# Post-FFN layer norm of a streaming encoder: where its two elementwise steps run

## The reference

```python
def layer_norm(x, g, b):
    xf = x.astype(jnp.float32)
    mu = jnp.mean(xf, axis=-1, keepdims=True)
    var = jnp.mean(jnp.square(xf - mu), axis=-1, keepdims=True)
    return ((xf - mu) * lax.rsqrt(var + LN_EPS) * g + b).astype(x.dtype)

def channel_and_ple(x, p, w13, w2, w_ple, w_gate, g, b):
    gate, up = jnp.split(x @ w13, 2, axis=-1)
    ffn = (jax.nn.silu(gate) * up) @ w2
    ple = jax.nn.sigmoid(x @ w_gate) * (p @ w_ple)
    return layer_norm(ALPHA * x + ffn + ple, g, b)
```

## Time and profile before

| | us |
|---|---|
| median of 3 runs | 3179.59 (3177.04 to 3186.04) |
| the profiled execution | 3180.57 |
| its span, first to last instruction | 3178.8 |
| TensorE busy | 3069.1 (97%) |
| VectorE busy | 1514.6 (48%) |
| ScalarE busy | 885.4 (28%) |
| GpSimd busy | 1016.3 (32%) |

### The profile page before, as it was taken

The page is one execution under the profiler, slowest core; times in us unless marked ns, Lnnn a source line. Parts: engine busy times, 40 slices in busy tenths (PEclk is TensorE's granted clock), DMA queues, the critical chain, the costliest instruction groups (busy, mean ns, idle before and its releaser), DMA issues.

```text
span 3178.8 us, 49155 instructions
## 1 busy us (share of the span) xinstructions
PE 3069.1 (97%) x19621; PEld 2881.9 (91%) x19621; DVE 1514.6 (48%) x2914; ACT 885.4 (28%) x1915; POOL 1016.3 (32%) x495
## 2 busy tenths in 40 slices
PE   8998999899999999999989999979999999999996
PEld 8697778789999999999979999967899999999996
DVE  1897855544533433333454554565444333333335
ACT  2575554342111001111134554553311111100112
POOL 3132000235633334333242222213545333333422
PEclk9998999899999999999999999989999999999998
DMA  3121000112311111111022111111222111111101
GB/s 101 28 64 38 1 1 1 41 50 81 92 46 46 46 40 53 46 46 40 14 70 58 50 43 47 40 47 54 73 89 60 52 43 45 45 46 40 53 0 55
DMA packets 209373, 149.75 MB, mean 47 GB/s; under 512 B 28914, under 2 KB 195764, under 8 KB 209236
## 3 DMA queue, kind: packets, MB, share of 16 engines
q1 hardware_dynamic: 209236, 147.85, 15.7%
HBM read 128.09 MB, written 19.73 MB: 47 GB/s over the span
## 4 chain that ended last, share of the span: by engine, by line
PE 89%; DVE 6%; issue 2%; ACT 2%; POOL 1%; DMA 0%; SPq 0%; POOLq 0%; ACTq 0%; DVEq 0%
PE psum L153 49%; PE psum L2130 16%; PE psum L1734 6%; PE psum L690 4%; PE psum L659 2%; PE psum L1322 2%; PE psum L1296 2%; DVE junk L913 2%; PE psum L671 2%; PE psum L1310 1%; PE psum L628 1%; DVE bias L872 1%; PE psum L1271 0%; PE psum L1688 0%; PE psum L1933 0%
## 5 line engine op out<-in xcount | busy, mean ns | idle before, releaser
L153 PE MATMUL psum<-x_hi,w_hi 128*128 128x352 f32 x3192 | 1039.4, 326 | 10.0 <-POOL x_lo L1677 4.1
L153 PE MATMUL psum<-x_hi,w_lo 128*128 128x352 f32 x3192 | 1026.1, 321 | 0.0
L153 PE MATMUL psum<-x_lo,w_hi 128*128 128x352 f32 x3192 | 1025.9, 321 | 0.0
L122 POOL TENSOR_TENSOR w_hi<-w_raw,zeros 128x1024 fp32r<-128x1024 f32 (+1 forms) x209 | 381.2, 1824 | 1514.6 <-PE psum L153 952.8
L153 PEld LDWEIGHTS psum<-x_hi,w_hi 128*128 128x128 f32 x3192 | 600.1, 188 | 12.2 <-issue 11.4
L153 PEld LDWEIGHTS psum<-x_lo,w_hi 128*128 128x128 f32 x3192 | 601.2, 188 | 0.5
L153 PEld LDWEIGHTS psum<-x_hi,w_lo 128*128 128x128 f32 x3192 | 599.7, 188 | 0.5
L124 POOL TENSOR_TENSOR w_lo<-w_raw,w_hi 128x1024 fp32r<-128x1024 f32 (+1 forms) x209 | 486.0, 2325 | 16.4
L2391 DVE TENSOR_TENSOR gate<-psum,gate 128x352 f32<-128x352 f32 x120 | 63.0, 525 | 725.3 <-PE psum L153 725.3
L2130 PE MATMUL psum<-h_hi,w_hi 128*128 128x352 f32 x1056 | 340.8, 323 | 1.2 <-DVE h_lo L2413 1.0
L2130 PE MATMUL psum<-h_lo,w_hi 128*128 128x352 f32 x1056 | 338.3, 320 | 0.0
(11 more groups left out here) (461 smaller groups left out, 4100.7 us busy)
## 6 DMA issues: line engine op xcount, KB each, us to landing
w_raw<-in_ffn_w_dram SPq DMA_DIRECT2D x132, 512.0 KB
w_raw<-in_b_w_in_dram SPq DMA_DIRECT2D x24, 512.0 KB
w_raw<-in_ple_w_gate_dram SPq DMA_DIRECT2D x16, 512.0 KB
x_nat<-in_x_prompt_dram SPq DMA_DIRECT2D x8, 512.0 KB, 7.6
w_raw<-in_a_w_in_dram SPq DMA_DIRECT2D x8, 512.0 KB
w_raw<-in_a_w_in_dram SPq DMA_DIRECT2D x16, 256.0 KB
x_rows<-x_rows SPq DMA_DIRECT2D x8, 512.0 KB, 2.8
out_new_b_v_prompt_dram<-valsB SPq DMA_DIRECT2D x8, 512.0 KB, 3.4
```

The costliest lines, as they stand in the source:

```text
L122: nc.gpsimd.tensor_tensor(c.w_hi[s][:, 0:kc], c.w_raw[s][:, 0:kc], zero, ALU.add).then_inc(c.split[s], 1)
L153: last = c.nc.tensor.matmul(out, w, x, start=(n == 0), stop=(n == 3 * len(terms) - 1))
```

## The change

The norm's elementwise work is arranged differently. Instead of (x/sd - mean/sd) * gain + shift in three passes on three engines, VectorE computes ((x - mean) * gain) from the PSUM rows in one scalar_tensor_tensor (`centered`), and then (that * 1/sd) + shift in a second one (`finished`), which follows its reciprocal. -mean/sd isn't computed any more; ScalarE's `normal` and GpSimd's `shifted` are gone. `centered` doesn't need the root. What `normal` waited for (the store of the buffer's last rows, and in layer 0 the turning back of tile t - 3) `centered` waits for now, on VectorE. PSUM places are free when `centered` is done (`s_gn`). In layer 1, tiles 7 and 8 get PSUM places of their own (banks 4 and 5, 6 and 7), so that TensorE turns them without a wait for an earlier tile, and tile 8 gets a fourth row buffer. The small buffers for statistics go from two to four. In the written order, `centered` and `finished` take the places of `coefs` and `gained`, with the last tiles in a slightly different order.

```diff
     def turn_bank(t):
+        if last_one and t > 6:
+            return 4 if t == 7 else 6
         return 2 if t in (5, 7) else 0
...
-        if before is not None:
-            pe.wait_ge(s_n, b_n + before + 1)
+        if before is not None and not (last_one and t > 6):
+            pe.wait_ge(s_gn, b_gn + before + 1)
...
     def stats(v, t):
-        n, j = rows(t), t % 2
+        n, j = rows(t), t % 4
         v.wait_ge(s_tr, b_tr + t + 1)
+        if t >= 4:
+            v.wait_ge(s_x, b_x + t - 3)
...
-        if t >= 2:
-            v.wait_ge(s_n, b_n + t - 1)
...
-    def coefs(v, t):
+    def centered(v, t):
+        n, j = rows(t), t % 4
+        v.wait_ge(s_mv, b_mv + t + 1)
+        if t >= 3 and not (last_one and t == QT):
+            v.wait_ge(s_out[t % 3], b_out + 16 * (t // 3))
+            if not last_one:
+                v.wait_ge(s_bt, t - 2)
+        nc.vector.scalar_tensor_tensor(out=xt[t][0:n, :], in0=c.psum[0:n, 512 * turn_bank(t):512 * turn_bank(t) + D],
+                                       scalar=mv[0:n, j, 0:1], in1=gain[0:n, :], op0=ALU.subtract,
+                                       op1=ALU.mult).then_inc(s_gn, 1)
+
+    def finished(v, t):
+        n, j = rows(t), t % 4
         v.wait_ge(s_sd, b_sd + t + 1)
         nc.vector.reciprocal(coef[0:n, j, 1:2], coef[0:n, j, 0:1]).then_inc(s_co, 1)
-        v.wait_ge(s_co, b_co + 2 * t + 1)
-        nc.vector.scalar_tensor_tensor(out=coef[0:n, j, 2:3], in0=mv[0:n, j, 0:1], scalar=-1.0,
-                                       in1=coef[0:n, j, 1:2], op0=ALU.mult, op1=ALU.mult).then_inc(s_co, 1)
-
-    def normal(act, t):
...
-    def gained(v, t):
...
-    def shifted(g, t):
...
+        v.wait_ge(s_gn, b_gn + t + 1)
+        v.wait_ge(s_co, b_co + t + 1)
+        nc.vector.scalar_tensor_tensor(out=xt[t][0:n, :], in0=xt[t][0:n, :], scalar=coef[0:n, j, 1:2],
+                                       in1=shift[0:n, :], op0=ALU.mult, op1=ALU.add).then_inc(s_x, 1)
...
@@ attention B, VectorE's order in layer 0 @@
         late.stats(v, 5)
         late.stats(v, 6)
-        late.coefs(v, 5)
+        late.centered(v, 5)
         late.low(v, 4)
-        late.coefs(v, 6)
-        late.gained(v, 5)
+        late.centered(v, 6)
+        late.finished(v, 5)
         late.stats(v, 7)
-        late.gained(v, 6)
-        late.coefs(v, 7)
-        late.gained(v, 7)
+        late.finished(v, 6)
+        late.centered(v, 7)
+        late.finished(v, 7)
         late.low(v, 5)
         project(0, K, 0)
         late.stats(v, 8)
         late.low(v, 6)
-        late.coefs(v, 8)
-        late.gained(v, 8)
+        late.centered(v, 8)
+        late.finished(v, 8)
         late.low(v, 7)
...
@@ feed-forward block, VectorE's order in the last pair @@
         added_last(2, (0,))
-        coefs(v, 4)
+        centered(v, 4)
         added_last(2, (1, 2))
-        gained(v, 4)
+        finished(v, 4)
         added_last(2, range(3, 8))
         if last_one:
             stats(v, 5)
             stats(v, 6)
-            coefs(v, 5)
-            coefs(v, 6)
-            gained(v, 5)
+            centered(v, 5)
+            finished(v, 5)
+            centered(v, 6)
             stats(v, 7)
-            gained(v, 6)
-            coefs(v, 7)
+            finished(v, 6)
+            centered(v, 7)
             stats(v, 8)
-            gained(v, 7)
-            coefs(v, 8)
-            gained(v, 8)
+            finished(v, 7)
+            centered(v, 8)
+            finished(v, 8)
```

More of the change, by code:

```diff
@@ L1863, in ffn_norm @@
     gate = c.at("gate" + tag, [P, 2, TOK], F32, 43008)
-    xt = [c.at(f"x_rows{j}_{tag}", [P, D], F32, (51456, 55552, 0)[j]) for j in range(3)]
+    row_tiles = [c.at(f"x_rows{j}_{tag}", [P, D], F32, (51456, 55552, 0, 4096)[j]) for j in range(3 + last_one)]
+    xt = [row_tiles[3 if last_one and t == QT else t % 3] for t in range(T)]
     gain, shift = c.at("gain_rows" + tag, [P, D], F32, 76032), c.at("shift_rows" + tag, [P, D], F32, 80128)
-    part = c.at("ln_part" + tag, [P, 2, 2, 6], F32, 84224)
-    mv, coef = c.at("ln_mv" + tag, [P, 2, 2], F32, 84352), c.at("ln_coef" + tag, [P, 2, 4], F32, 84384)
+    part = c.at("ln_part" + tag, [P, 4, 2, 6], F32, 84224)
+    mv, coef = c.at("ln_mv" + tag, [P, 4, 2], F32, 84416), c.at("ln_coef" + tag, [P, 4, 2], F32, 84448)
     S = lambda n: c.shared_sem("ffn_" + n)
@@ L2012, in ffn_norm @@
         late = c.late = Core()
-        late.turn, late.back, late.stats, late.root, late.coefs = turn_rows, turn_back, stats, root, coefs
-        late.normal, late.gained, late.high, late.low, late.rows_stored = normal, gained, high, low, rows_stored
+        late.turn, late.back, late.stats, late.root, late.centered = turn_rows, turn_back, stats, root, centered
+        late.finished, late.high, late.low, late.rows_stored = finished, high, low, rows_stored
         late.outputs_summed = lambda eng: eng.wait_ge(s_da, added(2, KC - 1))
@@ L2088, in pool @@
             split_unit(c, g, "attnB", 0, 1, KC)
-        for t in range(2, T):
-            shifted(g, t)
     def tensor(pe):
@@ L2304, in scalar @@
         root(act, 0)
-        normal(act, 0)
         high_last(0, 1)
         root(act, 1)
-        normal(act, 1)
         silu_last(1, 1)
@@ L2327, in scalar @@
         root(act, 4)
-        normal(act, 4)
         if last_one:
@@ L2331, in scalar @@
             root(act, 6)
-            for t in (5, 6):
-                normal(act, t)
-                root(act, t + 2)
-            normal(act, 7)
-            normal(act, 8)
+            root(act, 7)
+            root(act, 8)
     def vector(v):
@@ L2426, in vector @@
         stats(v, 0)
-        coefs(v, 0)
+        centered(v, 0)
         product_last(0, 1)
-        gained(v, 0)
+        finished(v, 0)
         low_last(0, 1)
         stats(v, 1)
-        coefs(v, 1)
-        gained(v, 1)
+        centered(v, 1)
+        finished(v, 1)
         if not last_one:
@@ L2441, in vector @@
         stats(v, 2)
-        coefs(v, 2)
+        centered(v, 2)
         product_last(0, 2)
-        gained(v, 2)
+        finished(v, 2)
         low_last(0, 2)
         stats(v, 3)
-        coefs(v, 3)
-        gained(v, 3)
+        centered(v, 3)
+        finished(v, 3)
         if not last_one:
```

29 lines of the change are left out of this document (6 added, 23 removed).

## The result

The changed kernel took 3164.44 us, median of 6 runs (3162.14 to 3166.22), against 3176.59 (3174.81 to 3186.04, 6 runs) for the kernel before: ratio 0.9950, 95% interval 0.9938 to 0.9962. The profiled execution took 3163.77, its span is 3162.0. The forecast was a gain of 13.3 us (0.42%); this comparison's ratio says 0.50%, some 16 us, its two medians 12.2 us (0.38%).

What follows compares the result with a forecast made beforehand. TensorE was taken as the bound (89% of the chain of waits). Layer 1's tail 8.5 us plus layer 0's hand-over 4.8 made 13.3 us, from a median of 3179.59 to 3166.3 us, range 3162 to 3173.

Steps and rivals of the forecast that it cites:

- What bounds, and the two places: TensorE carries 89% of the chain; the change acts only at layer 1's tail and layer 0's hand-over to attention B.
- The price of a pass: Each new VectorE pass of 1024 columns: 1.20 us start to start, 1.28 to its end, no PSUM surcharge.
- Part 1, the tail: End of layer 1: VectorE runs one unbroken queue, last norm pass ends at 3167.75 instead of 3176.22, gain 8.5 us.
- Part 2 (a): Layer 0, turning back tile 2: TensorE no longer waits for GpSimd's shift, 3.26 us of idle time go.
- (b): Layer 0, tile 3 turned back some 3.3 us earlier; the down product starts 2.8 us earlier.
- (c): Layer 0's down product: VectorE's queue stalls TensorE 1.0 us against 0.4, leaving 2.2 us of gain.
- (d): Layer 0, tile 5 to attention B's projection: 1.0 us less wait, 1.6 us by avoiding low clock, 2.6 us.
- microsecond of scatter between medians: Allowance used for the range 3162 to 3173, which was to take in R2 and R1.
- R1: Layer 0 gives nothing, through VectorE's longer queue or GpSimd's port collisions: gain 8.5 us, time 3171.1; chance 0.18.
- R2: Layer 0 gives nearly all its idle times hold, some 8 us: gain 16.5, time 3163; chance 0.12.
- R3: Slower: passes run at half rate; at 0.7 us more each the gain is gone, high end 3190; chance 0.05.
- R4: Another wait holds `centered` and TensorE's turns of tile 7 still wait: some 4 us gain, 3175.6; chance 0.07.

Runs made afterwards that it cites:

- e1: Changed kernel's norms and PSUM places in layer 1 only, layer 0 as in the kernel before: 3176.14 us, ratio 0.9991 to the kernel before.
- e2: Changed kernel's norms in layer 0 only, layer 1 as in the kernel before: 3174.63 us, ratio 0.9987 to the kernel before.
- e3: Changed kernel with the old PSUM places for tiles 7 and 8 of layer 1: 3166.34 us, ratio 0.9971 to the kernel before.
- x1: Kernel before, with layer 1's shift pass moved from GpSimd to VectorE behind the gain pass: 3180.00 us, one execution; tail 23.07 us.
- a1: Changed kernel again, no edit, in a second comparison: 3173.74 us, ratio 0.9969 to the kernel before.
- x2: Kernel before, with only the change's PSUM places for layer 1's last tiles: 3177.26 us, one execution; tail 24.81 us.
- a2: Changed kernel once more, no edit, in a third comparison: 3167.36 us, ratio 0.9963 to the kernel before.
- x3: Changed kernel plus an unneeded GpSimd pass beside each of tiles 5 to 8 in layer 1's tail: 3167.95 us, one execution; tail 22.87 us.
- x4: Changed kernel with another VectorE order in layer 0's attention B (finished of 5 and low of 5 earlier): 3170.72 us, one execution.
- x7: Same kernel as x6, timed in several runs: 3167.44 us, ratio 0.9939 to the kernel before.
- x5: x4 with 13 filler identity transposes on TensorE in place of the 1.42 us wait: 3159.99 us, one execution.
- x6: x4 with the tail's finishing of tiles 5 and 6 given to ScalarE and GpSimd: 3159.98 us, one execution; tail 14.99 us.

## Why the prediction was right, and where not

**What bounds, and the two places.** Right. Of the sections with touched code the tail and layer 0 alone moved by more than 0.15 us, and e1 and e2 show them one by one.

**The price of a pass.** Right. Both passes take 1.28 us and let the next start after 1.20. The step from reciprocal to `finished` was 0.20 to 0.26 us, forecast 0.18. No PSUM surcharge: `centered` (PSUM input) and `finished` (SBUF) take the same 1.28. My 544 ns for 512 more columns set a PSUM row beside an SBUF row of another length, so that by itself it couldn't have shown a surcharge.

**Part 1, the tail.** Right: 8.5 forecast, 8.3 measured, and 17.46 against the 17.3 that I gave as a check. The adds around tile 4's passes lost nothing (49.45 against 49.57). The claim that the places let VectorE run unbroken was wrong in its reason: e3 has the old places and the same tail. The row with 2.33 us was a collision, as said (x1).

**Part 2 (a).** Right: `finished` of tile 2 was held by the weight split, and TensorE didn't wait for it. VectorE's timeline, layer 0, against the gain pass of the earlier trace rows:

```profile
1589.08 2.39 DVE L1978 SCALAR_TENSOR_TENSOR x_rows<-x_rows,ln_coef,shift_rows 128x1024 f32<-128x1024 f32 x1
```

**(b).** Counted from X0, the down product starts 49.01 us in before (1607.69) and 45.60 after (1601.72): 3.4 earlier, forecast 2.8. The wait before tile 3's turning back is 1.47 (forecast about 1.0).

**(c).** Forecast 2.2 left at the end of this product; measured 57.80 - 55.14 = 2.7. From the down product's start to the last add it is 8.79 before and 9.54 after, 0.75 of new stall where I had 0.6.

**(d).** This is the step that failed. It had 2.6 us: 1.0 of waits and 1.6 of low clock that I took to be gone because TensorE's idle time fell from 2.44 to 1.75 us. Measured from the last add to T: 40.42 before, 39.65 after, 0.8. The waits, 1.82 + 2.44 + 1.42 before, are 1.63 + 1.90 + 1.42: 0.7 less, so that term is near. Up to V2 I am right even in size (30.93 to 28.58, 2.35; counted from X0, V2 comes 5.0 us earlier, forecast 4.8). But 1.6 us came back between V2 and T (9.49 to 11.07), one wait further on, so the 1.6 was worth nothing. In a1, the same kernel, the low clock sits where it did before:

```profile
1634.57 1.86 PE L1942 MATMUL psum<-ident,x_rows 128*128 128x128 f32 x8 [1.89 <-DVE x_lo L1993]
```

and V2 to T is 9.49; the sum is 94.9, against 94.8. All four profiles with the old layer 0 (before, e1, x1, x2) paid it behind the same wait of 2.44 or 2.45 us. The six with the changed one (the changed kernel, a1, a2, e2, e3, x3) paid it too: a1 behind the wait of 1.89 us, the other five one wait on, behind that of 1.42. So the shorter wait mostly moved the fall and never took it away. x4 and x7 paid it once as well, x5 and x6 not at all. I had read a cause into a single execution. Layer 0 gave 3.4 and not 4.8.

**The sum and the range.** 13.3 forecast, 11.8 by sections, of which the low clock explains 1.6: step (d) lost 1.8 and the tail 0.2, steps (b) and (c) gave 0.5 more. The comparison that came first said 0.50%, more than the trace can find in the touched code, and the next two 0.31 and 0.37%. The step behind this is my "microsecond of scatter between medians": single executions of one kernel lie from 3157 to 3177, and six runs fall into one group or the other. The first median, 3164.44, lies within my range of 3162 to 3173; a1's, 3173.74, of the same kernel doesn't, and that the first came so near to my 3166.3 is in part luck. Whatever the forecast's centre, a range from the terms of the sum alone was too sure of its upper and lower edge.

**The rivals.** R1 fell (layer 0 gave 3.4), though its mechanism is real: had GpSimd worked in the tail, 5.4 of 8.3 us would have gone (x3). R2 fell: the waits at tile 5, at `low` of 5 and of 8 stayed, 4.95 of 5.68 us. x4 shows that it was the order, not the price, that held them. R3 fell with the 1.28 us. R4 fell: nothing held `centered`, and TensorE turned tile 7 without a wait.

**Open.** What decides whether TensorE falls to the low clock at a given wait. The Trainium skill (TensorE: Matmul & The Clock Gate, Part 1) says that one and the same kernel gets different numbers of slow matmuls from run to run, because the chip's watch on activity isn't tied to the kernel's start; the pairs a1 and the changed kernel, x7 and x6 agree with that, but nothing here isolates it. x6 and x7 are the same kernel with the same waits (0.54, 0.38 and 1.42 us; 0.54, 0.38 and 1.41), without and with the low clock; they ran on different chips.

## What to carry to other kernels

Where several engines pass a row to one another behind the last product, work out what the whole chain costs on one engine with no hand-over: three passes and two hops became two passes of 1.28 us, for 8.3 us. When that engine has become the bound, give the others what has slack, and keep GpSimd away while the bound engine has instructions with two SBUF inputs (x6, x3). For a gain of less than 0.5%, cut the traces at shared instructions and compare sections; they repeat to 0.15 us where whole runs scatter by 19, apart from the low clock's 1.6 us.

## What the hardware showed that I had not expected

- Executions of one kernel on one chip scatter by up to 19 us (3157.27 to 3176.72 for a2). In the pair that I compared (a1 and the changed kernel) 7.3 of 10.1 us lie before the norms of layer 0, and the granted clock differs there: 0.74 against 0.89 from 290 to 350 us. The kernel's start differs too: the first two groups of 24 products in the chain of waits took 5.72 and 5.66 us in the kernel before, 4.47 and 4.08 in the changed one, from the same code.
- One dip to the low clock costs 1.6 us here, and which wait it follows changes between executions (a wait of 1.89 us in a1, of 1.42 in the changed kernel); it also came with waits of 0.53, 0.36 and 1.42 us (x4) and stayed away with 0.54, 0.38 and 1.42 (x6).
- A 1-column operation with two SBUF inputs is held by GpSimd's lock as a long one is: 0.16 us alone (x1), 2.33 beside a shift. The reciprocal, with one SBUF input, isn't: 0.11 us at 3152.04 in x3, within a GpSimd pass.
